# Seven products in place of eight in one quarter of a routed expert's first layer, with the weight differences on VectorE

## The chip, the cores and the metric

One core of one Trainium2 chip runs the whole program. The metric is the device time in microseconds (us); lower is better. Three runs of the kernel before took 1322.66, 1323.9 and 1325.47 us.

## What is computed

The reference is a two-layer decoder trunk on 256 tokens of width 1024: a gated linear recurrence and a dense SwiGLU, then sliding-window attention and a layer of routed experts (top 2 of 8). Only the experts matter here:

```
hid = jax.nn.silu(xb @ w_gate[e]) * (xb @ w_up[e])    # xb: tokens of expert e, 1024 wide; 3584 hidden columns
y   = hid @ w_down[e]                                 # back to 1024
```

All of it is float32. The three matrices of an expert are 3 x 1024 x 3584 x 4 bytes = 44.04 MB, and all eight are read.

## The kernel before

**The loop.** The expert layer is a loop of items; an item is one expert with up to 96 (`CAP`) of its tokens. With these inputs there are 8 items. The 96 tokens are three groups (`GRPS`) of 32 (`GTOK`). `xT[:, j, kt, :]` holds 32 tokens of group j for one slice `kt` of 128 of the 1024 input features (8 slices, `KT`).

**Four strips at once.** The tokens are the stationary operand, only 32 columns wide, so four matmuls lie side by side in TensorE, each with another quarter of the weight chunk's columns and another quarter of the output partitions (the loop over c in `up_products`, L1881). A float32 matmul shows as two MATMUL instructions, each with its LDWEIGHTS, in the trace.

**The stages of an item.** The 3584 hidden columns are two super-blocks (`SUPERS`): 4 x 384 and 4 x 512 columns. For each there is a gate phase (8 chunks, into banks 0 to 2) and an up phase (8 chunks, into banks 3 to 5). ScalarE takes Silu of the gate banks (L889), VectorE multiplies with the up banks (L1411) and transposes (L1415) into `hidT`. Then 14 down chunks (`down_products`, L1890) add up into banks 6 and 7, and ScalarE and VectorE copy the 96 x 1024 result to `yb` (L892 to L894, L1423, L1424), from where a DMA on ScalarE's queue stores it. VectorE also transposes the next item's tokens, `xr`, to `xT` (L1420).

**The weight ring.** The 46 chunks of an item (0 to 15 of 0.79 MB, 16 to 45 of 1.05 MB) go through a ring in SBUF that holds a third of an item, in the tiles `raw` and `more_ring`. SyncE issues them in order (L472, L475). Each waits (`wait_used`, L477) until TensorE has used the chunk that lay there one lap before: a count on `up_used` or `dn_used`. TensorE waits for each chunk on `load_full`. Chunks 24 to 31 are the up phase of the second super-block.

**Other queues.** GpSimd scatters the tokens during item 0, and in the last item (item 7) gathers the results of the experts before with four indirect DMAs into `early` (L600), scales and adds them (L605, L608). At the end TensorE, VectorE and SyncE combine and store the last item's rows (L1934 to L1940, L1433, L531).

The wait for banks 6 and 7 to be free stands in front of the down phase:

```
for i in range(N_DN):
    if i == 0:
        pe.wait_ge(yb_ready, n * 2 + 1)
```

Of the kernel before, what the change touches and what calls it, by code (L numbers as in the profile page):

```python
# [9 lines left out]
P = 128  # L10
# [38 lines left out]
SIGNALS = N_LOADS // 2  # L49

# [47 lines left out]
def build_program(nc, a, out):  # L98
# [44 lines left out]
    with ctx:  # L143
# [9 lines left out]
        with ExitStack() as over:  # L153

            early = sb(over, "early", [P, TT, 2, D])
# [5 lines left out]
        cols = sb(ctx, "cols", [P, 64])  # L161
        gain_row = sb(ctx, "gain_row", [P, D])
# [88 lines left out]
        s = ExitStack()  # L251
        e_silu = sb(s, "e_silu", [P, GRPS, 512])
# [125 lines left out]
        early_ready = sem("early_ready")  # L378
        early_added = sem("early_added")
# [44 lines left out]
        END_BANKS = [banks[1], banks[2], banks[5], banks[0]]  # L424
# [15 lines left out]
        def _(sp):  # L440
# [94 lines left out]
        def _(pool):  # L535
# [47 lines left out]
            for t in range(TT):  # L583
                for i in range(2):
                    for c in range(4):
                        pool.wait_ge(up_used, 8 * t + 4 * i + c + 1)
# [10 lines left out]
            for t in range(TT):  # L597
                for i in range(2):
                    at = bass.IndirectOffsetOnAxis(ap=early_slot[:, t, i:i + 1], axis=0)
                    nc.gpsimd.indirect_dma_start(out=early[:, t, i, :], out_offset=None, in_=slot_rows, in_offset=at).then_inc(fetched[t][i], 16)  # L600
            for i in range(2):
                for t in range(TT):
                    pool.wait_ge(fetched[t][i], 16)
                    rows = early[:, t, i, :]
# [6 lines left out]
        def _(act):  # L611
# [270 lines left out]
            with act.Fori(0, n_items) as n:  # L882
                for sup, (_, w) in enumerate(SUPERS):

                    act.wait_ge(up_used, n * N_UP + (2 * sup + 1) * KT)
                    if sup:
                        act.wait_ge(e_hid_ready, n * (2 * GRPS) + GRPS)
                    for j in range(GRPS):
                        nc.scalar.activation(e_silu[:, j, 0:w], banks[j][:, 0:w], ACT.Silu).then_inc(e_silu_ready, 1)  # L889

                act.wait_ge(dn_used, n * N_DN + N_DN)
                nc.scalar.activation(yb[:, 0:512], banks[6][0:CAP, :], ACT.Copy)  # L892
                nc.scalar.activation(yb[0:GTOK, 768:1024], banks[6][CAP:P, 0:256], ACT.Copy)
                nc.scalar.activation(yb[GTOK:2 * GTOK, 768:1024], banks[6][CAP:P, 256:512], ACT.Copy).then_inc(yb_ready, 1)  # L894
# [8 lines left out]
        def _(dve):  # L903
# [449 lines left out]

            every_choice = lambda ap: ap.rearrange("p t i -> p (t i)").unsqueeze(2)
# [49 lines left out]

            n_items = dve.value_load(items[0:1, 16:17], min_val=E, max_val=MAX_ITEMS)
            with dve.Fori(0, n_items) as n:
                for sup, (_, w) in enumerate(SUPERS):
                    dve.wait_ge(up_used, n * N_UP + (2 * sup + 2) * KT)
                    for j in range(GRPS):
                        dve.wait_ge(e_silu_ready, n * (2 * GRPS) + (GRPS * sup + j + 1))  # L1410
# [552 lines left out]
```

## Time and profile before

| | |
|---|---|
| median of 3 runs | 1323.9 us (1322.66 to 1325.47) |
| span of the profiled execution (first to last instruction) | 1321.3 us; its own time apart from the span is not among the times shown |
| the expert loop in it | from 444.1 us to 1312.9 us |
| busy in the span | TensorE 98%, VectorE 27%, ScalarE 19%, GpSimd 4% |
| granted TensorE clock, mean | 0.996 |

A busy share is the share of the span in which an engine worked at something. Matmuls overlap, so the pace of a phase is read from where its first matmul and the first one of the next phase start, not from the duration of one. PE is TensorE's matmul, PEld its weight load, DVE VectorE, ACT ScalarE, POOL GpSimd, SP SyncE, and a q behind it that engine's queue.

### The profile page before, as it was taken

What the parts mean: (1) busy time and instruction counts of PE and PEld (TensorE: products, weight loads), DVE (VectorE), ACT (ScalarE), POOL (GpSimd) and SP (SyncE); (2) the same over time, 40 slices, a digit from 0 to 9 for tenths busy, and PEclk for the clock granted to TensorE, in tenths of its full rate; (3) what the DMA queues carried; (4) which work ended last, traced back from release to release, by engine and by line L of the source; (5) the groups of instructions that cost most, each with busy time, mean ns of one, the idle gap of its engine ahead of it and who ended that gap; (6) DMA issues with size and microseconds to landing.
All of it is one profiled execution on the core that took longest, in us unless ns stands there. A gap on an engine that the chain in (4) does not pass through costs nothing.

```text
span 1321.3 us, 32549 instructions
## 1 busy us (share of the span) xinstructions
PE 1299.1 (98%) x14662; PEld 879.8 (67%) x14662; DVE 360.1 (27%) x539; ACT 246.4 (19%) x370; POOL 56.0 (4%) x50
## 2 busy tenths in 40 slices
PE   8999999999899999999999999999999999999998
PEld 8998899988767533555745655665574575566565
DVE  5875555554875401000000100100100010010011
ACT  5554544443743100000000000000000000000000
POOL 1001000000000320000000000000000000001600
PEclk9999999999999899999999999999999999999999
DMA  9866555565522899999999999999999999999992
GB/s 321 269 210 225 185 182 177 187 223 191 184 96 72 360 421 420 415 419 418 416 419 419 418 418 418 418 410 419 419 404 420 418 407 418 416 409 414 419 413 110
DMA packets 114199, 442.52 MB, mean 335 GB/s; under 512 B 9284, under 2 KB 55700, under 8 KB 83348
## 3 DMA queue, kind: packets, MB, share of 16 engines
q1 hardware_dynamic: 107904, 424.75, 81.5%
q10 hardware_dynamic: 4820, 11.53, 2.5%
q0 software_dynamic: 1344, 4.20, 0.8%
q8 instruction: 120, 1.97, 0.6%
q14 instruction: 11, 0.09, 0.0%
HBM read 434.12 MB, written 12.08 MB: 338 GB/s over the span
## 4 chain that ended last, share of the span: by engine, by line
PE 93%; DVE 3%; ACT 2%; issue 1%; DMA 0%; ACTq 0%; DVEq 0%
PE bank L1888 44%; PE bank L1900 22%; PE bank L1442 8%; PE bank L1444 8%; PE bank L1443 8%; PE bank L1689 1%; PE bank L1600 1%; DVE w_lo L916 1%; ACT w_hi L626 0%; PE bank L1865 0%; DMA const<-in_shape_constants 0%; ACT ht_hi L654 0%; PE bank L1744 0%; PE bank L1940 0%; DVE q_from L1100 0%
## 5 line engine op out<-in xcount | busy, mean ns | idle before, releaser
L1888 PE MATMUL bank<-more_ring,xT 128*32 128x512 f32 (+1 forms) x3456 | 341.0, 545 | 0.0
L1888 PEld LDWEIGHTS bank<-more_ring,xT 128*32 128x32 f32 x3456 | 164.2, 110 | 163.5 <-issue 84.4
L1888 PE MATMUL bank<-raw,xT 128*32 128x384 f32 (+1 forms) x2688 | 259.3, 532 | 0.7 <-DVE xT L1352 0.7
L1888 PEld LDWEIGHTS bank<-raw,xT 128*32 128x32 f32 x2688 | 122.4, 110 | 127.0 <-issue 76.6
L1411 DVE TENSOR_TENSOR e_hid<-e_silu,bank 128x384 f32<-128x384 f32 (+1 forms) x48 | 26.9, 616 | 542.3 <-PE bank L1888 542.3
L1900 PE MATMUL bank<-more_ring,hidT 128*32 128x256 f32 x3072 | 171.4, 379 | 0.0
L916 DVE TENSOR_TENSOR w_lo<-raw,w_hi 128x2048 fp32r<-128x2048 f32 x62 | 141.5, 2289 | 99.1 <-ACT w_hi L626 99.0
L1900 PEld LDWEIGHTS bank<-more_ring,hidT 128*32 128x32 f32 x3072 | 120.8, 110 | 46.4
L1442 PE MATMUL bank<-ht_hi,w_hi 128*128 128x256 f32 x464 | 129.4, 279 | 1.5 <-DVE ht_lo L930 1.5
L1900 PE MATMUL bank<-raw,hidT 128*32 128x256 f32 x2304 | 129.9, 379 | 0.0
L1444 PE MATMUL bank<-ht_hi,w_lo 128*128 128x256 f32 x464 | 128.9, 278 | 0.0
L1443 PE MATMUL bank<-ht_lo,w_hi 128*128 128x256 f32 x464 | 128.9, 278 | 0.0
L626 ACT ACTIVATE w_hi<-raw 128x2048 fp32r<-128x2048 f32 x62 | 118.6, 1918 | 38.7 <-PE bank L1444 38.3
L1900 PEld LDWEIGHTS bank<-raw,hidT 128*32 128x32 f32 x2304 | 91.0, 110 | 37.9 <-issue 0.6
L889 ACT ACTIVATE e_silu<-bank 128x384 f32<-128x384 f32 (+1 forms) x48 | 22.6, 544 | 392.8 <-PE bank L1888 392.8
L1442 PEld LDWEIGHTS bank<-ht_hi,w_hi 128*128 128x128 f32 x464 | 87.9, 189 | 2.5 <-issue 2.4
L1443 PEld LDWEIGHTS bank<-ht_lo,w_hi 128*128 128x128 f32 x464 | 87.9, 189 | 0.0
L1444 PEld LDWEIGHTS bank<-ht_hi,w_lo 128*128 128x128 f32 x464 | 87.9, 189 | 0.0
L892 ACT ACTIVATE yb<-bank 96x512 f32<-96x512 f32 x8 | 4.7, 593 | 441.6 <-PE bank L1900 441.6
L1442 PE MATMUL bank<-w_hi,ht_hi 128*128 128x256 f32 (+1 forms) x224 | 74.4, 332 | 3.7 <-DVE ht_lo L944 1.6
L1444 PE MATMUL bank<-w_hi,ht_lo 128*128 128x256 f32 (+1 forms) x224 | 73.2, 327 | 0.0
L1443 PE MATMUL bank<-w_lo,ht_hi 128*128 128x256 f32 (+1 forms) x224 | 72.9, 326 | 0.0
(284 smaller groups left out, 898.6 us busy)
## 6 DMA issues: line engine op xcount, KB each, us to landing
more_ring<-in_moe_w_up SPq DMA_DIRECT2D x64, 1024.0 KB, 16.2
more_ring<-in_moe_w_down SPq DMA_DIRECT2D x64, 1024.0 KB, 16.9
raw<-in_moe_w_gate SPq DMA_DIRECT2D x64, 768.0 KB, 15.5
more_ring<-in_moe_w_up SPq DMA_DIRECT2D x64, 768.0 KB, 15.8
raw<-in_moe_w_gate SPq DMA_DIRECT2D x48, 1024.0 KB, 16.1
raw<-in_moe_w_down SPq DMA_DIRECT2D x48, 1024.0 KB, 17.5
more_ring<-in_moe_w_gate SPq DMA_DIRECT2D x16, 1024.0 KB
raw<-in_hgrn_w_in SPq DMA_DIRECT2D x15, 1024.0 KB, 11.8
```

The costliest lines, as they stand in the source:

```text
L626: nc.scalar.activation(w_hi[:, slot, :], raw[:, slot_raw, :], ACT.Copy).then_inc(hi_ready, 1)
L889: nc.scalar.activation(e_silu[:, j, 0:w], banks[j][:, 0:w], ACT.Silu).then_inc(e_silu_ready, 1)
L892: nc.scalar.activation(yb[:, 0:512], banks[6][0:CAP, :], ACT.Copy)
L916: nc.vector.tensor_tensor(w_lo[:, slot, :], raw[:, slot_raw, :], plain(w_hi[:, slot, :]), SUB).then_inc(split_ready, 1)
L1411: nc.vector.tensor_tensor(e_hid[:, j, 0:w], e_silu[:, j, 0:w], banks[GRPS + j][:, 0:w], MUL).then_inc(e_hid_ready, 1)
L1442: nc.tensor.matmul(dst, st[0], mv[0], start=first, stop=False)
L1443: nc.tensor.matmul(dst, st[0], mv[1], start=False, stop=False)
L1444: return nc.tensor.matmul(dst, st[1], mv[0], start=False, stop=last)
L1600: whole = lambda bank_rows, at, w, st, mv: nc.tensor.matmul(bank[bank_rows:bank_rows + CH, at:at + w], st, mv, start=True, stop=True)
L1689: nc.tensor.matmul(LOGIT_BANKS[g % 2][b][:, :], const[:, K_ANTI:K_ANTI + P], bias_rev[:, GRP * g:GRP * g + GRP, :][:, heads, 2 * P - P * ( ...
L1888: ins = nc.tensor.matmul(out_banks[j][GTOK * c:GTOK * c + GTOK, 0:w], xT[:, j, kt, :], chunk[:, c], start=kt == 0, stop=kt == KT - 1)
L1900: ins = nc.tensor.matmul(banks[6 + j // 2][GTOK * c:GTOK * c + GTOK, 256 * (j % 2):256 * (j % 2) + 256], hidT[sup][:, g, m, :], ring_place ...
```

## The change

The up phase of the second super-block (chunks 24 to 31) is computed another way; everything else keeps its arithmetic. For the first two token groups (64 tokens) each pair of chunks, split into its left and right halves of columns, is a 2 x 2 block product (token group x feature slice, times feature slice x column half). Eight products of 32 tokens x 256 columns per strip become seven (P1 to P7), by Strassen's scheme in Winograd's form. They need four sums of tokens (`xsum`, made once per item by `token_sums`) and four differences of weights (`sums`, made by `weight_sums` for each pair, four VectorE operations of 128 x 1024). The third token group is still multiplied directly: four products of 256 columns (H1 and H2, two each). The four pairs add up in PSUM. `up_columns` then makes the up values out of the products, with ScalarE copying P1 first.

The products need banks 3 to 7, so the down phase moves from banks 6 and 7 to 1 and 2. The wait for those banks moves from the down phase to the beginning of the item: TensorE first multiplies only group 0 of chunks 0 to 2 (bank 0), then waits for `yb_ready`, then does groups 1 and 2 of the same chunks. The four end products move to banks 3 to 6. `early` becomes `xs` and a new tile, and `sums` takes its old place.

```diff
+FAST = (False, True)
...
-                    sp.wait_ge(up_used, n * N_UP + (m + 1))
+                    sp.wait_ge(up_used, n * UP_STEPS + UP_USED[m])
...
+            def weight_sums(n, sup, pair):
...
+                free(1)
+                nc.vector.tensor_tensor(t1, b12, b11, SUB).then_inc(sum_ready, 1)
+                free(2)
+                nc.vector.tensor_tensor(t3, b22, b12, SUB).then_inc(sum_ready, 1)
+                free(3)
+                dve.wait_ge(sum_ready, n * T_STEPS + (done + 1))
+                nc.vector.tensor_tensor(t2, b22, t1, SUB).then_inc(sum_ready, 1)
+                if pair:
+                    dve.wait_ge(up_used, n * UP_STEPS + (PHASE_END[2 * sup] + pair))
+                dve.wait_ge(sum_ready, n * T_STEPS + (done + 3))
+                nc.vector.tensor_tensor(t4, t2, b21, SUB).then_inc(sum_ready, 1)
...
+                        for pair in range(PAIRS):
+                            weight_sums(n, sup, pair)
+                        up_columns(n, sup)
...
+            def fast_products(n, sup, pair):
...
+                times("P1", xT[:, 0, k, :], b11)
+                times("P2", xT[:, 0, k + 1, :], b21)
+                if pair == 0:
+                    pe.wait_ge(xsum_ready, n * 4 + 4)
+                times("P3", xsum[:, 3, pair, :], b22)
+                times("H1", xT[:, 2, k, :], b11)
+                times("H1", xT[:, 2, k + 1, :], b21, False)
+                times("H2", xT[:, 2, k, :], b12)
+                times("H2", xT[:, 2, k + 1, :], b22, False)
+                pe.wait_ge(sum_ready, n * T_STEPS + (done + 1))
+                times("P5", xsum[:, 0, pair, :], t1).then_inc(sum_used, 1)
+                pe.wait_ge(sum_ready, n * T_STEPS + (done + 2))
+                times("P7", xsum[:, 2, pair, :], t3).then_inc(sum_used, 1)
+                pe.wait_ge(sum_ready, n * T_STEPS + (done + 3))
+                times("P6", xsum[:, 1, pair, :], t2).then_inc(sum_used, 1)
+                pe.wait_ge(sum_ready, n * T_STEPS + (done + 4))
+                times("P4", xT[:, 1, k + 1, :], t4).then_inc(up_used, 1)
...
+                        for kt in range(AHEAD):
+                            loaded(kt)
+                            up_products(banks, kt, w, (0,))
+                        pe.wait_ge(yb_ready, n * 2 + 1)
+                        for kt in range(AHEAD):
+                            up_products(banks, kt, w, (1, 2))
```

There is one set of four buffers in `sums`, so `weight_sums` can be at most one pair ahead. A pair's two chunks are given back to the ring together, with P4.

TensorE at the beginning of an item, before:

```order
L1922 ISA [waits x_ready]
L1888 MATMUL bank<-raw,xT 32x384 [waits load_full0]
L1888 MATMUL bank<-raw,xT 32x384 x11
L1888 MATMUL bank<-raw,xT 32x384 [waits load_full1]
L1888 MATMUL bank<-raw,xT 32x384 x11
```

The same place in the change:

```order
L2066 ISA [waits x_ready]
L2003 MATMUL bank<-raw,xT 32x384 [waits load_full0]
L2003 MATMUL bank<-raw,xT 32x384 x3
L2003 MATMUL bank<-raw,xT 32x384 [waits load_full1]
L2003 MATMUL bank<-raw,xT 32x384 x3
L2003 MATMUL bank<-raw,xT 32x384 [waits load_full2]
L2003 MATMUL bank<-raw,xT 32x384 x3
L2079 ISA
L2003 MATMUL bank<-raw,xT 32x384 [waits yb_ready]
L2003 MATMUL bank<-raw,xT 32x384 x23
```

Twelve matmuls now stand in front of the wait for `yb_ready`, and 24 that were spread over the first three chunks stand behind it.

TensorE on two chunks in the up phase of the second super-block, before (24 matmuls of 512 columns; `load_full` is numbered modulo 23):

```order
L1888 MATMUL bank<-more_ring,xT 32x512 [waits load_full3]
L1888 MATMUL bank<-more_ring,xT 32x512 x11
L1888 MATMUL bank<-more_ring,xT 32x512 [waits load_full4]
L1888 MATMUL bank<-more_ring,xT 32x512 x11
```

The same two chunks in the change, pair 1 (44 matmuls of 256 columns):

```order
L2021 MATMUL bank<-more_ring,xT 32x256 [waits load_full4,load_full3]
L2021 MATMUL bank<-more_ring,xT 32x256 x7
L2021 MATMUL bank<-more_ring,xsum 32x256 x4
L2021 MATMUL bank<-more_ring,xT 32x256 x16
L2034 REGISTER_ALU
L2021 MATMUL bank<-sums,xsum 32x256 [waits sum_ready]
L2021 MATMUL bank<-sums,xsum 32x256 x3
L2036 REGISTER_ALU
L2021 MATMUL bank<-sums,xsum 32x256 [waits sum_ready]
L2021 MATMUL bank<-sums,xsum 32x256 x3
L2038 REGISTER_ALU
L2021 MATMUL bank<-sums,xsum 32x256 [waits sum_ready]
```

Behind the last of these rows come three more matmuls, and then the fourth wait on `sum_ready` with P4's four. VectorE, which did nothing between the transposes of the first super-block and the end of this phase, has this for the pair:

```order
L1470 ISA [waits load_full4,load_full3]
L1473 TENSOR_TENSOR sums<-more_ring 128x1024 [waits sum_used]
L1470 REGISTER_ALU
L1475 TENSOR_TENSOR sums<-more_ring 128x1024 [waits sum_used]
L1470 REGISTER_ALU
L1477 REGISTER_ALU [waits sum_used]
L1478 TENSOR_TENSOR sums<-more_ring,sums 128x1024 [waits sum_ready]
L1480 REGISTER_ALU
L1481 REGISTER_ALU [waits up_used]
L1482 TENSOR_TENSOR sums<-sums,more_ring 128x1024 [waits sum_ready]
```

Each of the four stands behind a wait for TensorE, and the third and fourth behind one for VectorE's own result as well.

## Rows read from the trace of the kernel before

**Rows 1.** The page: span, busy time, clock and rate in 40 slices.

```profile
span 1321.3 us, 32549 instructions
PE 1299.1 (98%) x14662; PEld 879.8 (67%) x14662; DVE 360.1 (27%) x539; ACT 246.4 (19%) x370; POOL 56.0 (4%) x50
PEclk9999999999999899999999999999999999999999
GB/s 321 269 210 225 185 182 177 187 223 191 184 96 72 360 421 420 415 419 418 416 419 419 418 418 418 418 410 419 419 404 420 418 407 418 416 409 414 419 413 110
```

**Rows 2.** The chain that ended last: start, us, what.

```profile
444.11 72.46 PE bank L1888 x768
516.57 36.26 PE bank L1900 x672
...
1204.25 71.97 PE bank L1888 x762
1276.48 36.45 PE bank L1900 x668
```

**Rows 3.** Timeline, TensorE: first matmuls of a stretch (start us, us, engine, line).

```profile
588.92 0.61 PE L1888 MATMUL bank<-raw,xT 128*32 128x512 f32 x3
...
604.37 0.60 PE L1888 MATMUL bank<-more_ring,xT 128*32 128x512 f32 x3
...
624.97 0.39 PE L1900 MATMUL bank<-raw,hidT 128*32 128x256 f32 x3
...
640.51 0.39 PE L1900 MATMUL bank<-more_ring,hidT 128*32 128x256 f32 x3
...
661.23 0.50 PE L1888 MATMUL bank<-raw,xT 128*32 128x384 f32 x3
...
676.82 0.50 PE L1888 MATMUL bank<-more_ring,xT 128*32 128x384 f32 x3
```

**Rows 4.** Groups by line and shape, VectorE: operation, count, busy us, mean ns.

```profile
L1411 DVE TENSOR_TENSOR e_hid<-e_silu,bank 128x512 f32<-128x512 f32 x24 | 15.1, 682 | 305.4 <-PE bank L1888 305.4
L1267 DVE TENSOR_TENSOR pr<-pr,rsum 128x1024 f32<-128x1024 f32 x4 | 4.9, 1218 | 0.0
```

**Rows 5.** Timeline, VectorE behind an up phase of 512 columns.

```profile
625.87 1.88 DVE L1411 TENSOR_TENSOR e_hid<-e_silu,bank 128x512 f32<-128x512 f32 x3 [38.18 <-PE bank L1888]
627.79 1.90 DVE L1415 STREAM_TRANSPOSE hidT<-e_hid 128x512 f32<-128x512 f32 x3
```

**Rows 6.** Timeline, the copies of `yb` at the boundary of two items.

```profile
662.04 0.59 ACT L892 ACTIVATE yb<-bank 96x512 f32<-96x512 f32 x1 [55.20 <-PE bank L1900]
...
663.04 0.38 ACT L894 ACTIVATE yb<-bank 32x256 f32<-32x256 f32 x1
```

**Rows 7.** Stretches: us, busy us (instructions) by engine, PEclk, DMA share, GB/s.

```profile
560.00:660.00 100.00, 100.00 (x1335) 59.91 (x1330) 7.74 (x13) 2.83 (x6) 0.00 (x0) 1.00 1.02 418
...
1060.00:1160.00 100.00, 100.00 (x1361) 59.79 (x1354) 8.48 (x15) 4.18 (x9) 0.00 (x0) 1.00 1.01 414
...
1290.00:1292.00 2.00, 2.00 (x44) 1.47 (x39) 0.00 (x0) 0.00 (x0) 0.00 (x0) 1.00 0.49 205
```

**Rows 8.** DMA issues from 440, 1060 and 1236 us: size, median us to landing.

```profile
more_ring<-in_moe_w_up SPq DMA_DIRECT2D x8, 1024.0 KB, 15.4
...
more_ring<-in_moe_w_up SPq DMA_DIRECT2D x3, 1024.0 KB, 17.5
...
more_ring<-in_moe_w_up SPq DMA_DIRECT2D x2, 1024.0 KB, 24.0
```

**Rows 9.** Timeline, SyncE's issues of chunks 24 to 31, last item.

```profile
1223.99 17.09 SPq L472 DMA_DIRECT2D more_ring<-in_moe_w_up  x8
```

**Rows 10.** Timeline, TensorE in the last item, and GpSimd's first gather.

```profile
1255.28 0.60 PE L1888 MATMUL bank<-more_ring,xT 128*32 128x512 f32 x3
...
1275.88 0.39 PE L1900 MATMUL bank<-raw,hidT 128*32 128x256 f32 x3
...
1213.90 0.98 POOL L600 DMA_INDIRECT early<-slot_rows,early_slot  x1 [736.71 <-DMA slot_rows<-yb]
```

**Rows 11.** Issues of the last item's down chunks, SyncE: ns min/median/max, first and last start.

```profile
L475 SPq DMA_DIRECT2D more_ring<-in_moe_w_down x8: 333/333/333, 1262.0 to 1276.9; - x8
L475 SPq DMA_DIRECT2D raw<-in_moe_w_down x6: 333/1837/6193, 1243.3 to 1260.5; - x6
DMA to landing us min/median/max: 20.0/23.7/25.0
```

More of the change, by code:

```diff
@@ L49 @@
 SIGNALS = N_LOADS // 2
+FAST = (False, True)
+UP_USED, PHASE_END = [], []
+for _sup in range(2):
+    for _half in range(2):
+        _done = PHASE_END[-1] if PHASE_END else 0
+        _step = 2 if _half and FAST[_sup] else 1
+        UP_USED += [_done + kt // _step + 1 for kt in range(KT)]
+        PHASE_END.append(_done + KT // _step)
+UP_STEPS = PHASE_END[-1]
+PAIRS = KT // 2
+AHEAD = 3
+FAST_BEFORE = (0, PAIRS if FAST[0] else 0)
+T_STEPS = 4 * PAIRS * sum(FAST)
 def ring_offset(k):
@@ L153, in build_program @@
         with ExitStack() as over:
-            early = sb(over, "early", [P, TT, 2, D])
+            sums = sb(over, "sums", [P, 4, 4 * 256])
         ht_hi = sb(ctx, "ht_hi", [P, KT, T], f32r)
@@ L161, in build_program @@
         cols = sb(ctx, "cols", [P, 64])
+        with ExitStack() as over:
+            up_part = sb(over, "up_part", [P, 2, 256])
+            xsum = sb(over, "xsum", [P, 4, PAIRS, GTOK])
         gain_row = sb(ctx, "gain_row", [P, D])
@@ L599, in _ @@
                     at = bass.IndirectOffsetOnAxis(ap=early_slot[:, t, i:i + 1], axis=0)
-                    nc.gpsimd.indirect_dma_start(out=early[:, t, i, :], out_offset=None, in_=slot_rows, in_offset=at).then_inc(fetched[t][i], 16)
+                    nc.gpsimd.indirect_dma_start(out=early[i][:, t, :], out_offset=None, in_=slot_rows, in_offset=at).then_inc(fetched[t][i], 16)
             for i in range(2):
@@ L603, in _ @@
                     pool.wait_ge(fetched[t][i], 16)
-                    rows = early[:, t, i, :]
+                    rows = early[i][:, t, :]
                     then(nc.gpsimd.tensor_scalar(rows, rows, gate[:, t, i:i + 1], None, MUL))
@@ L1880, in _, with by_strip, up_products @@
                 gather(1, j)
-            def up_products(out_banks, i, w):
+            def by_strip(columns):
+                return columns.rearrange("p (m c i) -> p c m i", c=4, i=2 * GTOK)
+            def up_products(out_banks, i, w, groups=range(GRPS)):
                 kt = i % KT
-                chunk = ring_place(i).rearrange("p (m c i) -> p c m i", c=4, i=2 * GTOK)
-                for j in range(GRPS):
+                chunk = by_strip(ring_place(i))
+                for j in groups:
                     for c in range(4):
@@ L1889, in up_products, with times @@
                                                chunk[:, c], start=kt == 0, stop=kt == KT - 1)
-                ins.then_inc(up_used, 1)
+                if GRPS - 1 in groups:
+                    ins.then_inc(up_used, 1)
+            def fast_products(n, sup, pair):
+                w = SUPERS[sup][1]
+                b, k = w // 2, 2 * pair
+                first = 2 * KT * sup + KT + k
+                done = 4 * (FAST_BEFORE[sup] + pair)
+                (b11, b12), (b21, b22) = ((by_strip(ring_place(i)[:, 0:2 * w]), by_strip(ring_place(i)[:, 2 * w:4 * w]))
+                                          for i in (first, first + 1))
+                t1, t2, t3, t4 = (by_strip(sums[:, i, 0:2 * w]) for i in range(4))
+                def times(name, rows, columns, begin=True):
+                    dst, opens = piece(name, b), PLACES[name][2] and begin and pair == 0
+                    for c in range(4):
+                        ins = nc.tensor.matmul(dst[GTOK * c:GTOK * c + GTOK, :], rows, columns[:, c], start=opens,
+                                               stop=pair == PAIRS - 1, skip_group_check=True)
+                    return ins
+                times("P1", xT[:, 0, k, :], b11)
[15 more added lines that the diff above has]
+                times("P4", xT[:, 1, k + 1, :], t4).then_inc(up_used, 1)
             def down_products(i):
```

120 lines of the change are left out of this document (99 added, 21 removed).

## The prediction

> **What bounds the kernel now.** I read the page first: TensorE is busy 98% of the span at the full granted clock, and from slice 15 on the weights come at 404 to 421 GB/s [rows 1]. So two things are near their limit in the expert loop, and the question is which one gives way. The chain of waits is TensorE alone through all eight items: 72.46 us in the four up and gate phases and 36.26 us in the down phase, then the next item without a gap [rows 2]. From the end of the first item's up phases to that of the last it is (1276.48 - 516.57) / 7 = 108.56 us an item. TensorE waits for nothing, so time taken from it shortens the kernel, as long as its data are there.
>
> Paces come from where stretches begin [rows 3]. Six 512-wide chunks (144 instructions) take 604.37 - 588.92 = 15.45 us, 107.3 ns each. The up phase that is changed takes 624.97 - 604.37 = **20.60 us**. Six down chunks (288 instructions of 256 columns) take 15.54 us, 53.96 ns each. A 384-wide phase (192) takes 15.59 us, 81.2 ns each. VectorE is idle 305.4 us before 24 multiplies [rows 4], so it has room.
>
> Now the other limit. In an item 44.04 MB of weights and twice 0.39 MB of rows (`xr`, `yb`) move: 44.8 MB in 108.56 us, 413 GB/s. The stretches show 418 early and 414 late, at a DMA share of 1.02 and 1.01 [rows 7]: the stream is never idle and just keeps up. The times to landing say the same: 15.4 us, 17.5 us some 600 us later, and 24.0 us in the last item, after GpSimd's gather from 1213.90 on [rows 8, 10]. A chunk is issued about 31 us before its use: chunk 24 of the last item at 1223.99, used at 1255.28 [rows 9, 10]. So it lies ready for 31.3 - 24.0 = **7.3 us** there, against about 16 us in the first items. In the last item SyncE's issues themselves took up to 6.19 us where 0.333 us is usual [rows 11]: its queue is full. Near the end the rate is 205 GB/s at share 0.49 [rows 7], half of the engines being done before the others. A chunk lands with the slower half, which has had no pause. A faster TensorE therefore moves no landing forward: it only uses up the 7.3 us.
>
> **The products (TensorE).** Removed: 192 instructions, 20.60 us. Added: per pair 11 groups (seven products, four for token group 2) x 4 strips x 2 = 88 instructions of 256 columns, 352 in all, x 53.96 ns = 18.99 us. They have 21 waits where eight were; the down pace holds one per 48 instructions, seven here. The other 14 are not in the trace. Nearest row below: 53.96 ns against half of 107.3 ns, 0.31 x 48 = 15 ns a wait. Above: some 0.1 us, which makes 1.4 us. I take 0.02 us each, since nearly all of them should find their count already there: 0.3 us. Phase 19.3 us, **-1.3 us an item** (-1.6 to -0.2).
>
> **The weight differences (VectorE).** A 128x1024 tensor_tensor takes 1.218 us [rows 4]. Operations that don't need each other overlap a little: three of 0.682 us end after 1.88 us [rows 4, 5], start to start 0.60 us, 0.08 less than one lasts. So t1, t3 and t2 are 1.14 us apart; t4 needs t2's end and follows 1.26 us after it. With t4's overlap into the next t1 the period is 3 x 1.14 + 1.26 = 4.7; I take d = 4.75 us. TensorE needs 88 x 53.96 = 4.75 us for the pair: a dead heat. Pair 0's differences are made in the gate phase in front. t1 of pair 1 is released by P5 of pair 0: eight groups, 3.45 us, and 0.8 us until another engine sees it (the first matmul of an item starts at 661.23, the copies that wait for the one before it at 662.04 [rows 3, 6]). P4 of pair 3 starts about 0.1 us after its difference is ready and takes 0.43 us. So by VectorE the phase is 3.45 + 0.8 + 3d + 0.53 = 4.78 + 3d = 19.0 us, no more than by TensorE.
>
> In these rows back-to-back operations start before the one in front has ended. The Trainium skill ("VectorE: DVE Perf Modes", section on the DRAIN you can't avoid) says that the next one does not start until the pipe is empty. By that d = 4 x 1.22 = 4.9 and the phase 19.5 us, 0.2 us an item more, and 0.6 us more in the end (the last item, below, would run at 4.9 a pair). The rows decide for 4.75.
>
> **The wait at the item's start.** Before, `yb_ready` was awaited over 70 us late and cost nothing. Now the cover is 24 instructions x 81.2 ns = 1.95 us, until 663.18 on the clock of rows 3. The last copy ends at 663.04 + 0.38 = 663.42 [rows 6], so TensorE goes on at about 663.5: **+0.3 us** (0.1 to 0.5), seven times, since in the first item the banks are free. Behind the waiting matmuls is all of TensorE's queue.
>
> **At no cost.** `up_columns`: ScalarE's copy, seven operations of 256 columns and three of 512, none over the 0.68 us of a 512-wide one [rows 4], and the transposes at 1.9 us [rows 5], under 10 us in all; the down phase first uses the first super-block for six chunks, 15.54 us [rows 3]. If that cover were gone it would cost up to these 10 us an item. `xT` and the token sums (about 2 us more) are due only at the end of the 36 us. Chunks given back in pairs are issued 2.4 us later into a queue that is 15 to 31 us deep. The gather's other tile changes nothing.
>
> **The sum.** Without a limit from data: the last item starts 7 x (1.3 - 0.3) = 7.0 us earlier and its fast phase at 1255.28 - 7.0 = 1248.3. But chunk 25 lands at 1226.4 + 24.0 = 1250.4 (issues 2.4 us apart [rows 9]), and the first pair needs both. VectorE then needs four pairs: 1250.5 + 4 x 4.75 = 1269.5; by the last chunk, 1240.75 + 24.0 = 1264.8 plus 4.75, it is 1269.6. With P4 the phase ends at 1270.1 where it was 1275.88 [rows 10]: **5.8 us** earlier. Down chunks land 2.4 us apart and are used 2.6 us apart, so nothing more is lost, nor gained. The span goes from 1321.3 to 1315.5. The median of the runs is 2.6 us above that span; I put the same on top: **1318.1 us**. Hence the gain isn't 8.3 us (8 x 1.3 - 7 x 0.3): 2.5 us of it are left waiting for weights in the last item.
>
> **Rivals.** **(B) The stream has more to give.** If the backlog is only what TensorE's own pace lets build up, chunks land earlier when issued earlier and the whole 8.3 us come through: 1315.6 us. For it: stretches reach 421 GB/s [rows 1]. Against: share above 1, a full queue and a growing time to landing. The Trainium skill ("DMA: Bandwidth & Descriptors", "Where 436 GB/s comes from") gives 435 GB/s as the ceiling of the fabric; by that an item's 44.8 MB would take 103 us and B would be right. It also names about 358 GB/s for the HBM side, which this trace passes. No stretch here reaches 435.
>
> **(C) Many small losses.** Waits at 0.05 us (0.7 us), d = 4.9, 0.5 us at the start: 20.60 - 19.7 - 0.5 = 0.4 us an item, so 8 x 0.9 - 7 x 0.5 = 3.7 us: 1320.2 us, and the stream doesn't matter.
>
> **(D) VectorE is late.** The differences have up to two waits each on counts computed from the loop's number, and each pair runs through TensorE, VectorE and back. If these aren't covered, a difference costs 1.4 us where 1.19 was taken. From 4.78 + 3d = 20.60 - 0.3 the break-even is d = 5.17, 1.29 us each; it needs only 9% more. At d = 5.6 the phase is 21.6 us, +1.0 us, eight times, and 0.3 us seven times: +10 us, **1334 us**. Against: the multiplies of rows 5 have such waits too and start 0.60 us apart.
>
> **(E) It doesn't do what it says.** Seven for eight touches two of three groups of one of four phases, 1.3 of 108.6 us; losses of the same size in three places (waits, boundary, last item) cancel it: within 0.2%.
>
> **How the numbers follow.** A change of 0.2% (2.65 us) is about what a measurement of this kernel can tell from none. Forecast 0.47 (own range 1316.5 to 1319.7), B 0.19, C 0.16, D 0.12, E 0.06. B, the forecast and nearly all of C are faster: 0.78; slower 0.12; the same 0.10. The range 1315.0 to 1322.5 leaves out D and the far end of E and C.
>
> **What would show it.** The new phase about 19.3 us from first to last matmul in items 0 to 6; VectorE's operations of 1024 at 1.22 us, without gaps but before t4; a gap of about 0.3 us in TensorE, released by ScalarE, 2 us into items 1 to 7; in the last item a wait of some 2 us for chunk 25 and pairs at the pace of landings; the rate still 414 to 420. Wrong is the forecast if times to landing fall or the last item shows no wait (B), if PE waits for VectorE in every pair (D), or if the new phase is above 20 us (C).

## The result, and the profile after

The change makes the kernel slower: 1349.85 us (median of 4 runs, 1348.44 to 1351.22) against 1323.76 us (4 runs, 1322.66 to 1325.47), a ratio of 1.0195 with a 95% interval of 1.018 to 1.021. The forecast was 1318.1 us with a range of 1315.0 to 1322.5, so the sign is wrong, and the time by some 32 us. Yet the phase that the prediction was about came out as costed or better. The time was lost in a place for which it had no term.

The page of the changed kernel, for its span, the busy times, the rate in 40 slices and the queue that carries code:

```profile
span 1349.0 us, 35725 instructions
PE 1301.7 (96%) x15942; PEld 848.1 (63%) x15942; DVE 542.3 (40%) x759; ACT 249.3 (18%) x378; POOL 56.8 (4%) x50
GB/s 321 257 218 239 171 181 184 183 229 142 250 25 120 420 419 417 415 414 412 415 392 410 415 383 415 410 375 414 410 404 386 406 416 373 415 412 371 419 416 53
q8 instruction: 136, 2.23, 0.7%
```

Against [rows 1]: TensorE's busy time is 2.6 us longer and not shorter, its share fell by two points, and the rate, which never left 404 to 421 in the loop, now dips to between 371 and 392 about once an item. Two things follow: TensorE stands idle somewhere, and for some microseconds each time the stream slows too, since no ring places are given back. The chain of waits of the changed kernel (start, us, what) says where; the "issue" in it is time in which TensorE waited for nothing that the profile shows:

```profile
445.07 52.28 PE bank L2003 x576
497.35 18.99 PE bank L2021 x352
516.35 36.26 PE bank L2051 x672
552.61 3.83 issue
...
1005.53 53.46 PE bank L2003 x576
1058.99 18.99 PE bank L2021 x352
1077.98 36.26 PE bank L2051 x672
1114.24 3.60 issue
1117.84 53.46 PE bank L2003 x576
```

In [rows 2] the next item follows its predecessor's down phase without a gap. Here 3.1 to 3.8 us lie between them, seven times, 3.6 us on average. The changed phase itself takes exactly 352 x 53.96 ns = 18.99 us where 20.60 us stood, in six of the eight items of the chain. The stretches around one such gap (us, busy us of PE, PEld, DVE, ACT and POOL with their instructions, granted clock, DMA share, GB/s):

```profile
1002.00:1005.50 3.50, 0.00 (x0) 0.00 (x0) 0.74 (x2) 1.24 (x3) 0.00 (x0) 1.00 1.02 412
1005.50:1007.00 1.50, 1.47 (x12) 0.54 (x16) 0.00 (x0) 0.00 (x0) 0.00 (x0) 0.65 1.02 422
1007.00:1009.00 2.00, 2.00 (x17) 0.69 (x13) 0.00 (x0) 0.00 (x0) 0.00 (x0) 0.50 1.02 422
1009.00:1011.00 2.00, 2.00 (x28) 0.89 (x24) 0.00 (x0) 0.00 (x0) 0.00 (x0) 0.91 0.74 301
1011.00:1015.00 4.00, 4.00 (x54) 1.64 (x50) 0.00 (x0) 0.00 (x0) 0.00 (x0) 1.00 0.56 168
```

Behind the gap the granted clock is at 0.65, 0.50 and 0.91 for 5.5 us, 0.50 being the lower of the two levels, 1.2 GHz. Hence the 576 instructions of the first three phases take 53.46 us here; at full clock they take 51.56 us (below, in the first experiment). In six of the seven items behind a gap 1.7 to 3.1 us are lost this way; in the third item the clock stays at 1.00 behind a gap of 3.58 us, and why is not known. The stream runs on at 422 GB/s until the ring is full, and then falls to 301 and 168.

The sum fits the loop. An item is now (1303.48 - 516.35) / 7 = 112.45 us, where it was 108.56: a gap of 3.6, 1.9 for the clock (on average), 1.6 saved in the changed phase, together +3.9 us. Seven of these are 27 us, less the gain of the first item. The loop from its first matmul to its first end product (1341.23) takes 896.16 us, 25.9 more than the 870.29 of before (444.11 to 1314.40).

What does TensorE do in the gap? Its sequencer has one instruction there that is long. This is the view of one source line (engine, operation, count: ns min/median/max, first and last start), of the kernel before and then of the changed one:

```profile
L1911 PEldq COMPARE_BRANCH  x9: 88/452/493, 442.8 to 1311.2; - x9
```

```profile
L2062 PEldq COMPARE_BRANCH  x9: 88/4612/4857, 443.6 to 1338.1; - x9
```

It is the branch that closes the loop in TensorE's program, 452 ns before and 4612 ns now. The diff doesn't touch that loop:

```
25     LOOP_SLOT = 128
...
       with nc.Fori(0, n_items, engines=bass.OrderedEngineSet([pe.engine]), hint_back_edge=True,
                    head_slot={pe.engine: LOOP_SLOT}) as n:
```

What the diff changes is the loop's length. The page's queue of instructions shows that code comes by DMA, in packets of 2.23 MB / 136 = 16 KB, and during one item there are 14 of them, where the kernel before had 12. The Trainium skill ("Runtime: NRT & Kernel Launch", section on instruction fetch mechanics) says that an engine's code is refilled in blocks of 16 KiB, or 256 instructions, ahead of where it is, and that a taken branch to a target outside what is held waits for a fetch. The 16 KB of a packet agree with the first, and the branch of 4612 ns is what the second would look like. Counted in the programs, TensorE's loop body had 720 float32 products of 4 instructions and 13 others, 2893; it now has 800 x 4 + 33 = 3233. The loop's head is put at slot 128 of a block by `LOOP_SLOT`. So the closing branch was at slot (128 + 2893) mod 256 = 205 of its block, and is now at (128 + 3233) mod 256 = 33.

**Theory F** (fetch; the expectations below call it theory L): the fetch of the head starts when TensorE comes to the block that holds the branch; the later the branch lies in it, the more of the fetch is hidden. Then `LOOP_SLOT` alone decides, in either kernel. **Rival W**: the moved wait, the moved banks or the longer program as such (in the expectations rival N) make the pause. **Rival V**: VectorE or the stream do. A second question is the prediction's own: is the last item limited by the stream (**theory S**)?

### The profile page after: what moved, and what is told of

The parts are those of the page before. It is cut to its first block, busy times and chain, and to the rows that moved or that the text cites. A ratio compares the mean times of both kernels' runs of the same rounds, so it can differ in the third digit from the quotient of the medians.

```text
span 1349.0 us, 35725 instructions
## 1 busy us (share of the span) xinstructions
PE 1301.7 (96%) x15942; PEld 848.1 (63%) x15942; DVE 542.3 (40%) x759; ACT 249.3 (18%) x378; POOL 56.8 (4%) x50
## 3 DMA queue, kind: packets, MB, share of 16 engines
q8 instruction: 136, 2.23, 0.7%
## 4 chain that ended last, share of the span: by engine, by line
PE 92%; DVE 3%; issue 2%; ACT 2%; DMA 0%; ACTq 0%; DVEq 0%
PE bank L2003 32%; PE bank L2051 22%; PE bank L2021 11%; PE bank L1553 8%; PE bank L1555 7%; PE bank L1554 7%; PE bank L1800 1%; PE bank L1711 1%; DVE w_lo L955 0%; ACT w_hi L661 0%; PE bank L1976 0%; DMA const<-in_shape_constants 0%; ACT ht_hi L689 0%; PE bank L1855 0%; PE bank L2114 0%
## 5 line engine op out<-in xcount | busy, mean ns | idle before, releaser
L2003 PE MATMUL bank<-raw,xT 128*32 128x384 f32 (+1 forms) x2688 | 264.9, 551 | 26.0 <-issue 25.3
L2003 PEld LDWEIGHTS bank<-raw,xT 128*32 128x32 f32 x2688 | 98.6, 114 | 188.3 <-issue 175.2
L2003 PE MATMUL bank<-more_ring,xT 128*32 128x384 f32 (+1 forms) x1920 | 167.7, 507 | 0.0
L2051 PEld LDWEIGHTS bank<-more_ring,hidT 128*32 128x32 f32 x3072 | 112.8, 110 | 53.6
L2003 PEld LDWEIGHTS bank<-more_ring,xT 128*32 128x32 f32 x1920 | 66.9, 110 | 96.4 <-issue 92.8
L1520 DVE TENSOR_TENSOR e_hid<-e_silu,bank 128x384 f32<-128x384 f32 x24 | 11.9, 549 | 274.7 <-PE bank L2003 274.7
L2051 PEld LDWEIGHTS bank<-raw,hidT 128*32 128x32 f32 x2304 | 84.7, 110 | 39.9
L2021 PE MATMUL bank<-more_ring,xT 128*32 128x256 f32 x1536 | 101.2, 379 | 0.0
L1534 DVE COPY yb<-bank 96x256 f32<-96x256 f32 x8 | 3.4, 421 | 218.4 <-PE bank L2051 218.4
L1473 DVE TENSOR_TENSOR sums<-more_ring 128x1024 f32<-128x1024 f32 x32 | 39.2, 1225 | 126.9 <-PE bank L2021 124.4
```

What stands on the lines that cost most here:

```text
L1473: nc.vector.tensor_tensor(t1, b12, b11, SUB).then_inc(sum_ready, 1)
L2003: ins = nc.tensor.matmul(out_banks[j][GTOK * c:GTOK * c + GTOK, 0:w], xT[:, j, kt, :], chunk[:, c], start=kt == 0, stop=kt == KT - 1)
L2021: ins = nc.tensor.matmul(dst[GTOK * c:GTOK * c + GTOK, :], rows, columns[:, c], start=opens, stop=pair == PAIRS - 1, skip_group_check=True)
L2051: ins = nc.tensor.matmul(banks[1 + j // 2][GTOK * c:GTOK * c + GTOK, 256 * (j % 2):256 * (j % 2) + 256], hidT[sup][:, g, m, :], ring_place ...
```

## The experiments

**The loop's head moved, nothing else.** In `e1_head44`, `e3_head180` and `e4_head0` one number of the changed kernel differs, 44, 180 or 0 in place of 128; in `e2_before_head212` it is 212 in the kernel before. The diff of e1 stands for all:

```diff
-LOOP_SLOT = 128
+LOOP_SLOT = 44
```

Expected of e1:

> The change with TensorE's loop head at slot 44 of a fetch block instead of 128; nothing else. In the changed kernel the branch that closes an item takes 4.61 us (median) where it took 0.45 us before, TensorE is idle 3.6 us behind it, and then runs some us at half the granted clock. Theory L (place of the branch): a body of about 3233 instructions that begins at slot 128 ends at slot 33 of a block, too short behind the block's start for the hinted code to arrive; with the head at 44 the branch is at slot 205, where it was before. Then the branch takes about 0.45 us, no idle time of more than 0.3 us is left at an item's start, the clock stays at 1.0, and the time is 1312 to 1319 us: about 1318 if the weight stream binds in the last item as I predicted, about 1313 if it doesn't. Rival N (length): the longer body as such (3233 against 2893) defeats the hint; then the branch still takes 4.6 us and the time stays at about 1350 us. Rival W (waits): the gap comes from the wait for yb that was moved to the item's start; same time of about 1350 us.

Measured: 1318.46 us (8 runs, 1316.79 to 1321.93) against 1323.06 us of the kernel before (11 runs), a ratio of 0.9964 [0.9953, 0.9974]. The changed kernel, with its branch at slot 205 again, is faster than both, by 0.4% against the kernel before. The line's view and the chain of e1:

```profile
L2062 PEldq COMPARE_BRANCH  x9: 87/452/482, 446.2 to 1308.7; - x9
```

```profile
982.35 51.56 PE bank L2003 x576
1033.91 18.99 PE bank L2021 x352
1052.90 36.26 PE bank L2051 x672
1089.16 51.56 PE bank L2003 x576
```

452 ns to the nanosecond, no "issue" between items, full clock behind them, 106.81 us an item. All of the 5.5 us of gap and clock are gone, and with them rivals W, N and V as causes of it, since e1 keeps the wait, the banks, VectorE's work and the length of the program.

Expected of e2:

> The kernel before with the loop head at slot 212 instead of 128, so that its closing branch is at slot 33 of its block as in the changed kernel; nothing else. Theory L: the branch takes about 4.6 us instead of 0.45, TensorE is idle about 3.6 us at the start of items 1 to 7 and then runs at half clock for some us; seven times 3.6 + 1.8 = +38 us less what is hidden, about 1355 to 1362 us. Rivals N and W: nothing changes, 1324 us.

Measured: 1385.92 us, one run, even more than expected. The kernel before, unchanged but for that number, loses 63 us. The closing branch has a median of 4678 ns. TensorE's timeline in e2 at one boundary:

```profile
1027.70 3.69 PE L1888 MATMUL bank<-raw,xT 128*32 128x384 f32 x20 [3.36 <-issue]
1033.06 7.30 PE L1888 MATMUL bank<-raw,xT 128*32 128x384 f32 x88 [1.67 <-issue]
```

The branch takes what slot 33 foretells. The miss is in the second line: another pause after 20 matmuls. From a head at slot 212 only 44 instructions are left in its block, and the block behind it isn't there yet either. I had moved the branch by moving the head, and had counted only the branch's side. So e2 shows that the place of the loop in memory alone can cost the kernel before more than the change did, but not how much of it is the branch.

Expected of e3 and of e4:

> The change with the loop head at slot 180: closing branch at slot 85. Theory L with the time read from the two known places (4.6 us at slot 33, 0.45 us at slot 205, about 0.027 us per slot): the branch takes about 3.3 us, TensorE is idle about 2.3 us per item; 1330 to 1342 us, depending on whether the clock falls after so short a pause. Rivals N and W: 1350 us.

> The change with the loop head at slot 0: closing branch at slot 161. Theory L: the branch takes about 1.3 us, TensorE is idle about 0.4 us more per item than with slot 44, no fall of the clock; about 3 us over the run with slot 44. Rivals N and W: 1350 us.

Measured: e3 1351.24 us, e4 1323.43 us, one run each. Their line's views, and e3's chain at one boundary:

```profile
L2062 PEldq COMPARE_BRANCH  x9: 88/3332/3452, 443.6 to 1338.4; - x9
```

```profile
L2062 PEldq COMPARE_BRANCH  x9: 88/1256/5286, 442.2 to 1310.3; - x9
```

```profile
888.33 2.19 issue
890.52 3.42 PE bank L2003 x36
893.94 2.14 issue
896.08 50.44 PE bank L2003 x538
```

Both branches took the time that was expected of them. The time of e3 is a miss of 9 us, for the same reason as in e2: its head is at slot 180, with 76 instructions left, and a second pause follows. With the head at slot 0 there is none at the item's start. But e4's first entry into the loop, also a jump, took 5286 ns, which e1's did not, and its items take 107.9 us where 0.4 us more than e1's 106.81 were expected; the time is 5.0 us above e1's and not 3. Part of that is another pause, of 0.3 to 0.8 us in items 1 to 6, behind 81 matmuls of the down phase:

```profile
848.18 2.15 PE L2051 MATMUL bank<-raw,hidT 128*32 128x256 f32 x36 [0.69 <-issue]
```

By the count of instructions it lies where the eighth block of the body ends (8 x 256 = 2048). The packet with the next block's code starts there 6.2 to 6.7 us behind TensorE's entry to the block in front, where about 3 us is usual (below). Why it is late is open.

The four slots in one table. The down phase that runs ahead of the branch executes an instruction of any kind each 53.96 / 2 = 27.0 ns (one MATMUL and one LDWEIGHTS a step), so the time from entry to the branch's block is its slot times 27.0 ns:

| slot of the branch | kernels | from entry to branch, us | branch, us | sum |
|---|---|---|---|---|
| 33 | after, e2 | 0.89 | 4.61, 4.68 | 5.50, 5.57 |
| 85 | e3 | 2.30 | 3.33 | 5.63 |
| 161 | e4 | 4.35 | 1.26 | 5.61 |
| 205 | before, e1 | 5.54 | 0.45 | 5.99 |

The sum is constant, 5.5 to 5.6 us, until the branch comes so late that the fetch is over. That is what theory F says: the fetch begins at the entry to the block and takes some 5.6 us. The packets of the queue of instructions can be dated too. In the changed kernel TensorE enters a branch's block at 1000.47 - 0.89 = 999.58 us; from 999.6 to 1002.6 us that queue moves nothing, and from 1002.6 to 1003.7 us it has one packet:

```profile
q8 instruction: 1, 0.02, 5.8%
```

At the seven boundaries of each of the kernels before, after, e1, e3 and e4 this packet starts 2.9 to 3.3 us behind the entry, whether the branch is at slot 33, 85, 161 or 205, and takes 1.0 to 1.1 us; where TensorE waits, the branch ends 1.4 to 1.5 us behind the packet's end. So the fetch follows the entry to the block and not the branch. What happens in the 3 us before the packet moves no row shows.

**The parts of the change by themselves.** `b4_banks_only` has the moved wait, the moved banks and the new place of `early`, with the old eight products, no differences and chunks given back one by one. Its body has 2893 instructions, as before.

```diff
-FAST = (False, True)
+FAST = (False, False)
```

> FAST = (False, False) with head 128: the up phases as before, but the down products in banks 1 and 2, the wait for yb behind 24 matmuls of an item, the token sums made and not used. The body has 2893 instructions as before, so the branch is at slot 205. Expected from the forecast's term: +0.3 us for each of seven items, 1323 to 1326 us, with TensorE's pause released by ScalarE's last copy. If the wait is hidden: 1322 to 1324. The branch 0.45 us in either case; if the moved wait and not the branch's place made the changed kernel slow, about 1349 us.

Measured: 1327.36 us, one run, against 1324.43 us (7 runs, 1322.59 to 1328.54) of the kernel before in the same set. The branch takes 452 ns. An item is (1280.58 - 519.96) / 7 = 108.66 us against 108.56, and the loop began 2.4 us later in this execution than in [rows 2]. The time is above the 1323 to 1326 us that were expected, by less than that late beginning. So the moved wait and the banks cost 0.1 us an item at most, and not the 26 us. The waits of e1 agree (engine, who for whom: us in total, times, longest):

```profile
PEld bank L2003 <- ACT yb L933: 1.8, 7, 0.3
```

The wait at the item's start is there, seven times 0.26 us, but in front of weight loads, which run ahead of the matmuls: the 576 matmuls behind it take 51.56 us, where the paces of [rows 3] give 2 x 15.59 + 20.60 = 51.8 us for them.

`b3_both_super_blocks` computes the first super-block's up phase by seven products too, and `LOOP_SLOT` is set so that the branch (body 880 x 4 + 51) is at slot 205:

```diff
-LOOP_SLOT = 128
+LOOP_SLOT = 218
...
-FAST = (False, True)
+FAST = (True, True)
```

> FAST = (True, True): the up phase of the first super-block too by seven products, 192 columns wide, loop head at 218 so that the closing branch of the now longer body (about 3571 instructions) is at slot 205. TensorE alone would save another 15.6 - 352 x 40.6 ns = 1.3 us an item, 10 us. Theory S: the last landings don't move, so the time stays within 3 us of the 1318.5 us of head 44 (1316 to 1321), with longer waits for weights in the last items. Rival (no limit by the stream): about 1308 us. If VectorE, with differences of 768 columns (about 0.95 us) against 0.89 us of products each, falls behind, there are waits of TensorE for VectorE in the first up phase.

Measured: 1364.17 us (4 runs, 1359.07 to 1365.17), ratio 1.0284 [1.025, 1.0318]: a plain miss, and of the same kind as e2. The branch is short, and the pause has moved behind the head, after 17 matmuls, where 38 instructions of the block are used up (inside the new narrow phase there is another, of 1.8 to 2.1 us in most items):

```profile
1237.44 1.78 PE L2003 MATMUL bank<-raw,xT 128*32 128x384 f32 x17
1242.66 9.56 PE L2003 MATMUL bank<-raw,xT 128*32 128x384 f32 x116 [3.44 <-issue]
```

That left open whether two fast super-blocks lose for some other reason too. `d1_both_head0` puts the head at slot 0 and the branch at 243:

```diff
-LOOP_SLOT = 218
+LOOP_SLOT = 0
```

> FAST = (True, True) once more, with the loop head at slot 0 instead of 218. The run with head 218 took 1364 us although its closing branch took 0.45 us: TensorE paused 3.2 us some 0.7 us behind an item's start (the head's block held only 38 instructions) and again inside the first up phase. Theory L2 (a block's successor arrives about 5.7 us after the block is entered, so a head late in its block starves as a branch early in its block does): with the head at 0 and the branch at slot 243 the pause at the item's start is gone. Then what is left: Theory S (stream): 1317 to 1322 us, 4 of them from a slow entry into the loop as in the run with head 0. Theory F (in the phase 192 columns wide 256 instructions last only 64 x 81.2 ns = 5.2 us, less than the 5.7 us): TensorE still pauses inside that phase, up to 2 us an item, 1320 to 1335 us. If neither head nor width matters: 1364 us.

Measured: 1336.89 us (4 runs, 1335.3 to 1338.8), ratio 1.0102 [1.0077, 1.0126], 2 us above the range of the narrow-phase theory, which this expectation alone calls theory F. The pause at the item's start is gone, and items take about 108.4 us, but without any pause they would take 105.5 us: e1's 106.8, less 15.59 us of a 384-wide phase [rows 3] plus 352 steps of 40.6 ns (below), 14.3 us. Most of the rest is inside the new phase, whose products are 192 columns wide: 16.9 us in the item shown. TensorE's timeline there:

```profile
907.38 0.53 PE L2021 MATMUL bank<-more_ring,xT 128*32 128x192 f32 x8 [0.87 <-issue]
...
908.05 1.48 PE L2021 MATMUL bank<-more_ring,xT 128*32 128x192 f32 x32
909.35 1.16 PE L2021 MATMUL bank<-sums,xsum 128*32 128x192 f32 x24
...
913.81 0.68 PE L2021 MATMUL bank<-more_ring,xT 128*32 128x192 f32 x10 [1.03 <-issue]
```

From 907.38 to the next pause at 912.8 is 5.4 us, and 256 instructions at this pace are 5.2 us: 32 matmuls and their weight loads from 908.05 to 909.35, 40.6 ns a step, 20.3 ns an instruction. TensorE uses up a block faster than the 5.6 us in which one comes. So straight code too can wait for its own fetch, where its instructions are short enough. At 256 columns, 27 ns an instruction or 6.9 us a block, no run shows such a pause of over 0.1 us in the changed phase; e4's pause in the down phase, at the same pace, shows that this width is no safeguard.

**VectorE's share.** `d2_fifth_difference` is e1 with a fifth operation in each pair, whose result nobody uses:

```diff
+                nc.vector.tensor_tensor(e_hid[:, 0:2, :].rearrange("p j c -> p (j c)"), b11, b21, ADD)
                 free(1)
                 nc.vector.tensor_tensor(t1, b12, b11, SUB).then_inc(sum_ready, 1)
```

> The change with head 44 and a fifth VectorE operation of 128x1024 per pair, unused, ahead of t1. From the forecast's 4.78 + 3d with d = 4.75 + 1.14 = 5.89 us: the new phase takes 22.4 us instead of 18.99, 3.5 us more in each of eight items, TensorE waiting for VectorE before the later products; the stream then no longer binds, so 1310.3 (the run with the light stream) + 28 = about 1338 us. If VectorE has real room: 1318 us unchanged.

Measured: 1321.0 us, one run, where e1's median was 1318.46 and 1338 was expected; TensorE now waits for VectorE, so an item takes 108.4 us and not 106.8. Its waits, and the piece of its chain ahead of the second half of the phase:

```profile
PE bank L2022 <- DVE sums L1483: 7.5, 16, 0.6
```

```profile
711.18 13.86 PE bank L2022 x256
```

The down phase follows at 731.75, so the phase takes 731.75 - 711.18 = 20.57 us instead of 18.99: +1.6 us, where my formula gave 3.5. The fifth operation of the first pair is made ahead of the phase, and that of the second in the time in which VectorE waits for TensorE's release; the formula had three full periods of five. TensorE starts its pairs at 711.00, 715.74, 720.49 and 725.77 us and the down phase at 731.57: the first two take their 4.75 us, the third 5.3 and the fourth 5.8, which is VectorE's own period with five operations. So there is a margin, but one for the phase and not one a pair: in e1 the fourth difference is ready 0.6 us before its products start (731.25 against 731.85 us in the last pair of an item), in pairs 1 to 3 alike, and one operation more a pair uses it up.

**The stream.** In e1 the items before the last take 106.81 us and the last one 1310.1 - 1196.0 = 114.1 us. Its timeline has what the prediction looked for, TensorE waiting for chunks of the second super-block's up weights (2.3 us), and as much again in two phases ahead of it, which the prediction did not have:

```profile
1252.20 1.07 PE L2021 MATMUL bank<-more_ring,xT 128*32 128x256 f32 x16 [1.55 <-DMA more_ring<-in_moe_w_up]
...
1258.37 1.07 PE L2021 MATMUL bank<-more_ring,xT 128*32 128x256 f32 x16 [0.76 <-DMA more_ring<-in_moe_w_up]
```

and the DMA queues of e1 from 1215 to 1240 us (packets, MB, share of 16 engines; then issue, count, size, median us to landing):

```profile
q1 hardware_dynamic: 1333, 9.20, 88.4%
q0 software_dynamic: 354, 1.25, 12.5%
...
more_ring<-in_moe_w_up SPq DMA_DIRECT2D x7, 1024.0 KB, 27.4
```

Three kernels test it. `b2_head44_light` is e1 with half of the columns of the first eight chunks of an item left unloaded; `b1_before_light` has the same edit on the kernel before, as a control.

```diff
-                if k < N_UP:
+                if k < KT:
+                    half = 2 * SUPERS[0][1]
+                    sp.dma_start(ring_place(k)[:, 0:half], up_source(e, k)[:, 0:half]).then_inc(load_full[k % SIGNALS], 16)
+                elif k < N_UP:
```

> Control. The kernel before, where SyncE loads only half the columns of each of the first eight chunks of an item (the gate chunks of the first super-block); the products use what lay in the other half, so the gate values of the first super-block are wrong. That takes 3.1 MB of 44.8 MB out of every item's stream and leaves TensorE's work as it was. If TensorE alone bounds the kernel before, 1321 to 1325 us. If the stream already holds it back, it gets faster by more than 3 us.

> The change with the loop head at 44, and the same lighter stream (half the columns of the first eight chunks of an item aren't loaded; gate values of the first super-block wrong). Theory S (with the branch in its place, the stream is what holds the last item back): the item period is 106.8 us as in items 3 to 6 of the run with head 44, all eight items keep it, TensorE waits for no weights, 1309 to 1312 us against 1318.5. Rival (the rest of the expected gain is lost elsewhere, in the item's start or on VectorE): 1318 us as with the full stream.

Measured: b1 1326.28 us, with a loop of 872.80 us against 870.29: fewer weights gain the kernel before nothing, so TensorE alone bounds it. (The time is 1 us above the expected range, and its loop is even longer, with five pauses of 0.2 to 0.5 us, whose cause is open.) b2 1310.29 us, with a loop of 857.84 us against e1's 863.91. The last item is as short as the others. A piece of b2's chain (start, us, what):

```profile
871.18 51.49 PE bank L2006 x573
922.67 18.84 PE bank L2024 x348
...
977.99 2.23 PE bank L2006 x25
```

`d3_head44_no_gather` keeps all weights and takes GpSimd's four gathers away:

```diff
-                    nc.gpsimd.indirect_dma_start(out=early[i][:, t, :], out_offset=None, in_=slot_rows, in_offset=at).then_inc(fetched[t][i], 16)
+                    nc.gpsimd.memset(early[i][:, t, :], 0.0).then_inc(fetched[t][i], 1)
```

> The change with head 44, and GpSimd's four gathers in the last item replaced by memsets to zero, so that the rows of all experts but the last item's aren't added (the output lacks them). That takes 2.1 MB out of the stream in the last item. Theory S: chunks 24 to 31 of the last item land about 5 us earlier, TensorE's waits for weights in the last item shrink from 6.5 us by about 5, and the time is 1312 to 1314 us. If the gather isn't what deepens the backlog: 1318 us.

Measured: 1312.69 us, with a loop of 859.05 us. One wait for an up chunk of that phase is left:

```profile
PE bank L2021 <- DMA more_ring<-in_moe_w_up: 0.7, 1, 0.7
```

So theory S holds: of the 6.1 us that the stream costs e1 in its last item (863.91 - 857.84), the gather makes 4.9 (863.91 - 859.05). In the 25 us shown above it moves 1.25 of its 2.1 MB while the weights move 9.20 MB, and takes 12.5% of the engines' time for it. The light stream also moves the packets of code sooner: in b1 they start 1.6 to 2.0 us behind the entry to the branch's block and in b2 1.8 to 3.1 us, where 2.9 to 3.3 us are usual, so a part of those 3 us seems to be the weights' doing.

## Why the prediction was wrong, point by point

**The step that failed** is in its first paragraph: "then the next item without a gap". That was read off [rows 2] as a property of TensorE's queue, and it is the property of one number of that program, the slot of the closing branch. The sum had a term for every wait the change adds, and none for the 340 instructions it adds to the loop's body. The runs put 3.1 to 3.8 us of idle time in its place, seven times, and in six of these 1.7 to 3.1 us of lower clock behind it. The COMPARE_BRANCH of 452 ns and the 120 packets of code were in the trace of before, and `head_slot` was in the code, a hand-set number that fits one body length. It should have been a rival at least: "the loop is longer, so the place of its branch moves". None of the five rivals was it. D had the right sign by the wrong mechanism, and E's losses "in three places" were too small.

**The products: right.** 352 x 53.96 ns = 18.99 us was measured to the last digit. The 0.3 us that I put on top for 14 waits was not there: a wait whose count is reached costs nothing that these rows show. The saving is 1.61 us an item, where 1.3 was taken.

**The weight differences: right.** The dead heat was one that TensorE won. VectorE's timeline in the changed kernel, over one pair and the beginning of the next:

```profile
726.06 1.22 DVE L1473 TENSOR_TENSOR sums<-more_ring 128x1024 f32<-128x1024 f32 x1 [15.99 <-PE bank L2021]
727.20 1.22 DVE L1475 TENSOR_TENSOR sums<-more_ring 128x1024 f32<-128x1024 f32 x1
728.33 1.22 DVE L1478 TENSOR_TENSOR sums<-more_ring,sums 128x1024 f32<-128x1024 f32 x1
729.59 1.23 DVE L1482 TENSOR_TENSOR sums<-sums,more_ring 128x1024 f32<-128x1024 f32 x1
730.81 1.23 DVE L1473 TENSOR_TENSOR sums<-more_ring 128x1024 f32<-128x1024 f32 x1
```

The starts are 1.14, 1.13, 1.26 and 1.22 us apart, 4.75 us in all, the d that was taken. It is TensorE's pace, though: the last of these steps holds a wait for it, and in d2, where VectorE sets the pace, that step is 1.14 us, so four operations alone would take 4.67. Operations of 1.22 us that start 1.14 us apart overlap, which is what the rows of before said. By the sentence of the Trainium skill that the prediction took ("VectorE: DVE Perf Modes", on the DRAIN you can't avoid) the four would need 4.9 us, and the measurement decides against that. But the same section goes on that a next operation that is not "held", its word for one that has to wait for those in front, starts earlier, and with that the overlap agrees: the prediction read only half of it. The margin is 0.6 us ahead of a pair's last product, and d2 uses it up.

**The wait at the item's start: too high**, 0.3 us where nothing to 0.1 us came. I saw the weight load's wait, and not that it runs ahead of the matmul.

**The last item: right in kind, too small.** With the branch put right the changed kernel runs in 1318.46 us, and the forecast said 1318.1, but that is luck, since two errors cancel in it. By the loops of the profiled executions the gain of TensorE's work is 870.29 - 857.84 = 12.5 us and not 8.3, and the stream takes 6.1 us of it back and not 2.5; 6.4 us remain where 5.8 were forecast. (By the medians of one set of runs, 1323.06 and 1318.46, it is 4.6.) The loss came out larger because the last item starts 4.9 us sooner than I had it (11.9 us earlier in the loop than before, where 7.0 were taken), and because the time to landing did not stay at 24.0 us but went to 27.4: a queue that is asked earlier is only deeper. Rival B is refuted by these numbers: chunk 24 of the last item is issued 775.5 us into e1's loop, 4.4 us earlier than before (779.9), and chunks 24 to 31 take 3.8 us longer to land (27.4 against 23.6), so that they land hardly earlier.

**Right, and without consequence:** `up_columns`, `token_sums` and the changed giving back of chunks cost nothing that shows.

## What to carry to other kernels

Where a long loop is closed by a jump, the length of its body is a quantity of its own: read the branch's row in the sequencer, count the instructions that a change adds, and see where in its block the branch comes to lie and how much of the head's block is left behind the head. A number in the code that places a loop is tuned for one body, and a change of the body is a change of it; set it again before judging the change. A gap in TensorE's work can cost more than its length, in the changed kernel half as much again on average, since the clock is lower behind most of them.

## What the runs showed that I had not expected

The closing branch took 4.61, 3.33, 1.26 and 0.45 us at slots 33, 85, 161 and 205 of its block. A head late in its block makes a pause once the rest of the block is used up: 0.4 to 2.1 us at slot 180, 1.7 to 2.4 at slot 212, 3.1 to 3.4 at slot 218. Straight code of 20 ns an instruction outruns its own fetch, by 0.87 and 1.03 us in the item shown, and in e4 even code of 27 ns paused once an item. Two pauses of about 2 us each an item, in e3, cost clock (1.7 us) in only four of seven items. A jump into the loop at slot 0 took 5.3 us once, in e4, and 6.4 us in d1.

Open are four things. What the granted clock does behind a pause was only read, not varied. All the kernels give a hint for the branch (`hint_back_edge`, a BRANCH_PREFETCH_HINT of 35 ns at each item's start); no run leaves it out, so what it saves is not known. The loop began between 442.3 and 447.7 us in different executions with the head not at slot 0, more than some effects here, and why wasn't looked into. And no `LOOP_SLOT` was found for two fast super-blocks at which all of their pauses vanish; since the 192-wide phase outruns its fetch, one may not exist, but that wasn't tried.
